# Four score rows in one arena, and the indexer's transposes and split moved ahead, in the first stage of a hybrid attention layer

## The chip, the cores and the metric

The kernel runs on one core of a Trainium2 chip. The metric is the device time of one execution in microseconds (us); lower is better.

## The reference

One layer over 4096 prompt frames and 8 streams of 16 new frames. A projection makes queries, keys, values and gates of two head groups and the queries, keys and weights of a small indexer. Group A attends in a sliding window. Group B attends, for each query, to the 256 keys that the indexer scores highest:

```
h = rms_norm(x, norm_g);  p = h @ w_in
qa, ka, va, ga, qb, kb, vb, gb, qi, ki, wi = split(p)
r = relu(einsum('bqhe,ble->bqhl', qi, ki_all))       # 4 indexer heads of 64
score = einsum('bqhl,bqh->bql', r, wi)               # -inf on chunks that are not admissible
_, idx = top_k(score, 256)
o_b = softmax(q . k[idx] / 8 + bias[idx]) . v[idx]
y = concat(o_a * silu(ga), o_b * silu(gb)) @ w_out;  x = x + y
```

## The kernel before, in words

The program has three stages, one behind the other: `stage_one` (projection, indexer scores, search of the 256th score, masks), `stage_two` (attention of the prompt) and `stage_last` (the samples and the output projection). The change is in `stage_one` alone and in the tables that order it.

Stage one handles 32 tiles of 128 prompt frames and one of samples. Each engine has one instruction stream that is written out by hand. A step t has 12 slots, and what an engine does in a slot is decided by comparing planned times: `us_at(t, slot)` is the planned time of a slot, and VectorE and ScalarE weave their two kinds of work by it. They have a foreground, the tests of a search, and a background (a generator that yields a planned time ahead of each piece); `advance` issues the background pieces whose planned time has passed. So the planned costs only set the order; at run time every engine works strictly in that order and waits on semaphores.

TensorE (PE) in step t: the scores of row u = t - 1 in units of 512 columns spread over slots 0 to 7 (`score_units`, L614: 4 heads of two matmuls a unit, into 4 banks), the transposes of the keys and queries of tile t - 1, and the projections of tile t (L596): k/v in slot 0, qa 2, qb 4, the index group 6; from tile 10 on the gates `ga` and `gb` in slots 8 and 10; from tile 23 on also the gates of an early tile (t - 23) in 9 and 11. In slots 5 and 7 it transposes the two halves of x of tile t + 1, and in slot 9 the index queries (L578) and index key (L581) of tile t. The key's bank is free only when ScalarE has copied the second half of x (L670).

ScalarE (ACT): evacuates each projection one slot later (L700; L698 for the index group), copies transposed pieces (L722, L725 for the index ones, in the slot behind theirs), takes the relu of the scores (L737, 3 buffers), and in its foreground searches the even rows with 31 tests over the whole row (L807).

GpSimd (POOL): weighs and adds the relus into the score row (L908 first head, L910 and L913 the others), marks the row ready with a memset (L917), and does the head norms.

VectorE (DVE): searches the odd rows with 32 tests (L1043), sums squares of heads (L946), splits the index query into a rounded part and a remainder (`split_q` L956, `split_k` L961; PE's scoring waits for both), and closes each row, even ones with the threshold that ACT found: a count (L993), two compares (L969, L970), a running sum over ties (L972), and two mask operations (L977, L980). The semaphore `s_fin` says that a close no longer needs its score row.

Score rows lie in three buffers, row a in `score[a % 3]`; POOL's first unit of row u waits until row u - 3 is closed:

```python
if j == 0 and u >= 5:
    pool.wait_ge(s_fin, u - 4)
```

Of the kernel before, what the change touches and what calls it, by code (L numbers as in the profile page):

```python
# [23 lines left out]
P = 128  # L24
# [101 lines left out]
N_PROJ = 2176  # L126
SLOTS = 12
RELU_GAP = 1.8
BIG = float(2 ** 100)
TESTS = 32  # L130
SEARCHED = TILES - 2
# [25 lines left out]
def unit_slot(u, j):  # L157

    return j * 8 // len(units(u))


SCORED = {}
# [47 lines left out]

def dve_us(t, slot):

    return 3.4 * (slot == 6) + 1.2 * (slot == 11) if t <= TILES else 0.0


def step_us(t):
# [67 lines left out]
def stage_one(nc, x_prompt, x_sample, norm_g, w_in, q_norm_a, k_norm_a, q_norm_b, k_norm_b,  # L284
# [3 lines left out]
    with ExitStack() as ctx:  # L288
# [14 lines left out]
        qi = sb("qi", [P, 2, IDX_HEADS * P], F32R)  # L303
        kiT = sb("kiT", [P, SEQ], F32R)
        relu = [sb(f"relu_{i}", [P, STEP]) for i in range(3)]
        score = [sb(f"score_{i}", [P, n]) for i, n in enumerate((31 * P, 32 * P, 30 * P))]
        mask = sb("mask1", [P, SEQ], BF16)
        ties = sb("ties", [P, 4 * PV], mybir.dt.int8)
        act_junk = sb("act_junk", [P, 31 * P], mybir.dt.int8)
# [22 lines left out]
        t_bank = [bank[:, (2 + i) * STEP:(3 + i) * STEP] for i in range(2)]  # L332
        s_bank = [bank[:, (4 + i) * STEP:(5 + i) * STEP] for i in range(4)]
        square = ties[:, :].bitcast(F32)
        bias_in, hot_in, ramp_sb = score[1][0:BUCKETS, 0:2 * HEADS], score[1][0:BUCKETS, STEP:STEP + 383], score[1][0:2 * HEADS, 2 * STEP:2 * STEP + 383]
        heads20 = proj[:, 0:PV].rearrange("p (h d) -> p h d", d=HD)

        s_const = sem("constants_loaded")
# [38 lines left out]
        block = ctx.enter_context(nc.Block())  # L377

        def row_of(a):
            return score[a % 3][:, 0:(a + 1) * P]  # L380

        @block.sync
        def _(sp):
# [67 lines left out]
            for t in range(TILES + 2):  # L451
                if t == 2:
                    sp.wait_ge(s_rampc, 1)
                    sp.dma_start(ramp[:, :, 0:RAMP - 1].rearrange("i h n -> h i n"),
                                 ramp_sb.unsqueeze(1).to_broadcast([2 * HEADS, P, RAMP - 1])).then_inc(s_ramps, 16)
                if t >= 1:
                    chosen_until(us_at(t, 1))
                    sp.wait_ge(s_tc, PIECE["k", t - 1] + 1)
                    from_ring(qk_t[t - 1, :, 2 * STEP:2 * STEP + 2 * P], P, 2 * P)
                    store_q(0, t - 1)  # L460
                if t < LATER:
                    sp.wait_ge(s_tc, PIECE["x1", t] + 1)
                    sp.dma_start(xt[t], x[t % 2][:, :]).then_inc(s_xt, 16)
                e = later_tile(t)
                if e is not None:
                    if e >= 1:
                        sp.wait_ge(s_pg, PROJ["gb", e - 1] + 1)
                    sp.dma_start(x_later[:, :], xt[e]).then_inc(s_xl, 16)
                if t <= TILES:
                    rows = slice(t * P, (t + 1) * P)  # L470
                    sp.wait_ge(s_ev, PROJ["kv", t] + 1)
                    sp.dma_start(values[t, :, 0:2 * P], proj[:, PV:PV + 2 * P]).then_inc(s_kv, 16)
                    if t < TILES:
                        sp.dma_start(b_v_prompt[0, 0].rearrange("t h d -> t (h d)")[rows], proj[:, PV + P:PV + 2 * P]).then_inc(s_kv, 16)
                    else:
                        sp.dma_start(b_v_sample[0].rearrange("b t h d -> (b t) (h d)"), proj[:, PV + P:PV + 2 * P]).then_inc(s_kv, 16)
                chosen_until(us_at(t, 4))
                if t >= 1:
                    store_q(1, t - 1)
                if t - 2 in LATE_TILES:  # L480
                    store_late(t - 2)
                if t > TILES:
                    continue
                chosen_until(us_at(t, 7))
                sp.wait_ge(s_ev, PROJ["idx", t] + 1)
                if t < TILES:
                    sp.dma_start(b_kidx_prompt[0, 0][rows], proj[:, PKI:PKI + HD]).then_inc(s_ki, 16)
                else:
                    sp.dma_start(b_kidx_sample[0].rearrange("b t d -> (b t) d"), proj[:, PKI:PKI + HD]).then_inc(s_ki, 16)
                chosen_until(us_at(t, 9))  # L490
                if t >= LATER:
                    sp.wait_ge(s_ev, PROJ["ga", t] + 1)
                    from_ring(gates[t, :, 0:STEP])
                if e is not None:
                    sp.wait_ge(s_ev, PROJ["ga", e] + 1)
                    from_ring(gates[e, :, 0:STEP])
                if t == TILES:
                    sp.wait_ge(s_tc, PIECE["iq", t] + 1)
                    from_ring(qi_new, HD)
                    sp.wait_ge(s_tc, PIECE["ik", t] + 1)  # L500
                    from_ring(ki_new, HD, P)
                sp.wait_ge(s_kn, t + 1)
                sp.dma_start(values[t, :, 2 * P:3 * P], proj[:, PK:PK + P]).then_inc(s_kv, 16)
                if t < TILES:
                    sp.dma_start(b_k_prompt[0, 0].rearrange("t h d -> t (h d)")[rows], proj[:, PK + P:PK + 2 * P]).then_inc(s_kv, 16)
                else:
                    sp.dma_start(b_k_sample[0].rearrange("b t h d -> (b t) (h d)"), proj[:, PK + P:PK + 2 * P]).then_inc(s_kv, 16)
                chosen_until(us_at(t, 11))
                if t + 2 <= TILES:
                    sp.wait_ge(s_pg, PROJ["gb" if t >= LATER else "idx", t] + 1)  # L510
                    if t < LATER:
                        sp.wait_ge(s_xt, 16 * (t + 1))
                    nxt = x_prompt[0, (t + 2) * P:(t + 3) * P] if t + 2 < TILES else x_sample.rearrange("b t d -> (b t) d")
                    sp.dma_start(x[t % 2][:, :], nxt).then_inc(s_x[t % 2], 16)
                if t >= LATER:
                    sp.wait_ge(s_ev, PROJ["gb", t] + 1)
                    from_ring(gates[t, :, STEP:2 * STEP])
                if e is not None:
                    sp.wait_ge(s_ev, PROJ["gb", e] + 1)
                    from_ring(gates[e, :, STEP:2 * STEP])  # L520
                if t == TILES:
                    sp.dma_start(a_k_sample[0, :, WINDOW - DEC:].rearrange("b t h d -> b t (h d)"), proj[:, PK:PK + P]).then_inc(s_last, 16)
                    sp.dma_start(a_v_sample[0, :, WINDOW - DEC:].rearrange("b t h d -> b t (h d)"), proj[:, PV:PV + P]).then_inc(s_last, 16)
                    sp.dma_start(wi_new, weight[:, t % 2, :]).then_inc(s_last, 16)
# [11 lines left out]
        def _(pe):  # L536
# [63 lines left out]
            def score_units(u, slot):  # L600

                for j, (c, n) in enumerate(units(u)):
                    if unit_slot(u, j) != slot:
                        continue
                    if j == 0:
                        pe.wait_ge(s_lo, 2 * u + 2)
                    for h in range(IDX_HEADS):
                        at = SCORED[u] + IDX_HEADS * j + h
# [11 lines left out]
            for t in range(TILES + 2):  # L620
                for slot in range(SLOTS):
# [9 lines left out]
                        transpose_q(1, t - 1)  # L631
                    if slot in (5, 7) and t < TILES:
                        transpose_x((slot - 5) // 2, t + 1)
                    if slot == 9 and t <= TILES:
                        transpose_indexer(t)
                    for at, name, of in groups_of_step(t) if t <= TILES else ():
                        if at == slot and slot > 0:
# [3 lines left out]
        def _(act):  # L641
# [97 lines left out]
            def background():  # L739
# [5 lines left out]
                for t in range(TILES + 3):  # L745
                    for slot in range(SLOTS):
                        before, b = divmod(SLOTS * t + slot - 1, SLOTS)
                        yield us_at(t, slot)
                        if b == 0 and 1 <= before <= TILES + 1:
                            copy_piece("k", before - 1)  # L750
                        for at, name, of in groups_of_step(before) if 0 <= before <= TILES else ():
                            if at == b:
                                evacuate(name, of)
# [5 lines left out]
                            copy_x((b - 5) // 2, before + 1)  # L759
                        if slot == 4 and t < TILES:  # L760
                            square_x(t + 1)
                        if b == 9 and before <= TILES:
                            copy_piece("iq", before)
                            copy_piece("ik", before)
                        if 3 <= t <= TILES:
                            for h, _ in enumerate(relu_unit(t - 1, slot)):
                                yield us_at(t, slot + 0.6) + RELU_GAP * h
# [92 lines left out]
        def _(pool):  # L860
# [31 lines left out]
            def add_scores(u, slot):  # L892
                last = len(units(u)) - 1
                for j, (c, n) in enumerate(units(u)):
                    if unit_slot(u, j) != slot:
                        continue
                    to = row_of(u)[:, c:c + n]
                    if j == 0 and u >= 5:
                        pool.wait_ge(s_fin, u - 4)
                    if j == 0 and u == 4:  # L900
                        pool.wait_ge(s_ramps, 16)
                    for h in range(IDX_HEADS):
                        at = SCORED[u] + IDX_HEADS * j + h
# [26 lines left out]
        def _(dve):  # L930
# [73 lines left out]
            def background():  # L1004

                taken = 2
                for t in range(TILES + 5):
                    for slot in (0, 3, 6, 9, 11):
                        while taken < SEARCHED and FOUND_AT[taken] <= us_at(t, slot):
                            yield FOUND_AT[taken]  # L1010
                            choose_act(taken)
                            taken += 2
                        if slot == 6 and t <= TILES:
                            yield us_at(t, slot)
                            sum_heads(t)
                        if slot == 11 and t < TILES:
                            yield us_at(t, 10.3)
                            split_q(t)
                            split_k(t)
                yield FAR_AWAY - 1  # L1020
                while taken < SEARCHED:
                    choose_act(taken)
                    taken += 2
# [1510 lines left out]
```

## Time and profile before

| | |
|---|---|
| time, median of 3 runs | 5097.78 us (5093.58 to 5100.38) |
| the profiled execution: its time, its span | 5096.76 us, 5095.0 us |
| first stage, from the start to the second stage's first instructions | 2456.4 us |
| busy, share of the span: PE, DVE, ACT, POOL | 85%, 69%, 68%, 32% |
| TensorE's granted clock, mean over the span | 0.92 of full speed |

A busy share is an average over all three stages. Idle time of an engine costs something only where another engine, or its own later work, waits for it. A wait that the trace puts down to "issue" is one whose releaser it does not show.

### The profile page before, as it was taken

To read this page: it belongs to the slowest core of one execution; us is meant where nothing else is said; L and a number is where in the kernel's file an instruction comes from. 1 tells how busy PE (TensorE), PEld (TensorE's weight loads), DVE (VectorE), ACT (ScalarE), POOL (GpSimd) and SP (SyncE) were. 2 spreads that over 40 slices of the span, in tenths; PEclk is the share of its full clock that TensorE was granted. 3 is DMA by queue.
4 is the path that set the end of the run, shared out by engine and by line. 5 is a ranking of instruction groups with operands and counts; after the bars stand their busy time and mean duration, and the time that the engine had idled before them with its cause. 6 is when DMAs were issued, how large, how long until landed. Compare 5 with 4: busy or idle time off the path is not lost. (4 is left out here: it accounts for less than half of the span.)

```text
span 5095.0 us, 78325 instructions
## 1 busy us (share of the span) xinstructions
PE 4347.4 (85%) x26505; PEld 2718.1 (53%) x26505; DVE 3499.8 (69%) x6644; ACT 3443.3 (68%) x6887; POOL 1619.9 (32%) x1358
## 2 busy tenths in 40 slices
PE   6777888777677786767689999989999999989999
PEld 3344444434343343434366777767777777754444
DVE  1277779888797898989477777787777778625111
ACT  1588888888787798872488888858788885520100
POOL 1345566667557757777210000000000000000000
PEclk8888889888788898978799999999999999999999
DMA  5211111100010111101421111011010010044422
GB/s 143 70 44 45 38 39 40 37 35 28 33 42 33 37 45 38 36 32 48 157 72 58 44 51 40 28 54 41 25 42 25 28 40 26 10 126 132 117 93 103
DMA packets 201975, 276.98 MB, mean 54 GB/s; under 512 B 50496, under 2 KB 134176, under 8 KB 201056
## 3 DMA queue, kind: packets, MB, share of 16 engines
q1 hardware_dynamic: 198624, 271.81, 16.9%
q8 instruction: 220, 3.60, 0.3%
q14 instruction: 171, 1.40, 0.1%
q10 hardware_dynamic: 2960, 0.17, 0.0%
HBM read 156.73 MB, written 114.16 MB: 53 GB/s over the span
## 5 line engine op out<-in xcount | busy, mean ns | idle before, releaser
L596 PE MATMUL bank<-w,x 128*128 128x512 f32 (+1 forms) x2848 | 1258.6, 598 | 19.2 <-DVE w L941 12.8
L1043 DVE TENSOR_SCALAR_CACHE_REDUCE ties<-score,cand 128x512 int8<-128x512 f32 (+13 forms) x448 | 1110.6, 2479 | 122.1 <-POOL score L917 106.7
L596 PEld LDWEIGHTS bank<-w,x 128*128 128x128 f32 x2848 | 576.9, 206 | 608.6 <-issue 549.7
L807 ACT ACTIVATE act_junk<-score,a_cand,a_sign 128x384 int8<-128x384 f32 (+13 forms) x420 | 879.4, 2094 | 14.0
L614 PE MATMUL bank<-kiT,qi 128*128 128x512 f32 (+3 forms) x1136 | 396.5, 489 | 450.5 <-ACT relu L737 244.9
L1834 DVE CUSTOM_DVE_ANT_0 row<-bank,mask 128x512 f32<-128x512 f32 (+3 forms) x1024 | 622.6, 639 | 181.6 <-PE bank L1573 180.3
L1540 POOL TENSOR_TENSOR near_bias<-table,mask 128x2048 f32<-128x2048 f32 (+1 forms) x32 | 129.5, 4047 | 1767.8 <-DVE part L1834 1751.4
L1768 ACT ACTIVATE pT<-bank 128x512 f32<-128x512 f32 (+2 forms) x704 | 368.4, 523 | 428.5 <-PE bank L1589 426.6
L1670 ACT ACTIVATE row<-row,top 128x1024 f32<-128x1024 f32 (+7 forms) x640 | 632.9, 990 | 4.0 <-DVE top L1847 4.0
L1573 PE MATMUL bank<-kT,qb 64*128 64x256 f32 (+1 forms) x4352 | 609.6, 397 | 9.0 <-DVE part L1834 5.6
L1589 PE MATMUL bank<-ident,row 128*128 128x128 f32 x4224 | 594.6, 281 | 26.4 <-DVE pT L1945 19.6
L1945 DVE COPY pT<-bank 128x512 f32<-128x512 f32 (+2 forms) x704 | 425.2, 604 | 255.8 <-PE bank L1589 254.2
L1618 PE MATMUL bank<-pT,v 128*64 128x128 f32 x8448 | 590.0, 280 | 0.0
L913 POOL TENSOR_TENSOR score<-score,relu 128x512 f32<-128x512 f32 (+3 forms) x426 | 560.3, 1315 | 33.4
L614 PEld LDWEIGHTS bank<-kiT,qi 128*128 128x128 f32 x1136 | 237.6, 232 | 578.3 <-ACT relu L737 307.0
L1618 PEld LDWEIGHTS bank<-pT,v 128*64 128x64 f32 x8448 | 450.9, 137 | 171.1 <-issue 163.7
L910 POOL TENSOR_TENSOR relu<-relu,weight 128x512 f32<-128x512 f32 (+3 forms) x426 | 499.3, 1172 | 76.9 <-ACT relu L737 76.7
L1589 PEld LDWEIGHTS bank<-ident,row 128*128 128x128 f32 x4224 | 453.1, 141 | 132.2 <-issue 97.0
L737 ACT ACTIVATE relu<-bank 128x512 f32<-128x512 f32 (+3 forms) x568 | 297.7, 554 | 252.1 <-POOL score L913 177.0
L2290 PE MATMUL bank<-wo,mix_in 128*128 128x512 f32 x1024 | 450.9, 599 | 0.0
L1573 PEld LDWEIGHTS bank<-kT,qb 64*128 64x128 f32 x4352 | 380.3, 187 | 125.5 <-issue 72.1
L908 POOL TENSOR_TENSOR score<-relu,weight 128x512 f32<-128x512 f32 (+3 forms) x142 | 164.6, 1159 | 651.4 <-issue 527.9
(255 smaller groups left out, 4900.1 us busy)
## 6 DMA issues: line engine op xcount, KB each, us to landing
qk_t<-ring SPq DMA_DIRECT2D x66, 256.0 KB, 2.0
gates<-ring SPq DMA_DIRECT2D x66, 256.0 KB, 2.0
gate<-gates SPq DMA_DIRECT2D x33, 512.0 KB, 3.4
out<-x_in SPq DMA_DIRECT2D x33, 512.0 KB, 2.9
x<-in_x_prompt SPq DMA_DIRECT2D x32, 512.0 KB, 3.7
mixed<-mixT SPq DMA_DIRECT2D x64, 256.0 KB, 2.0
mix_in<-mixed SPq DMA_DIRECT2D x32, 512.0 KB, 4.3
x_in<-in_x_prompt SPq DMA_DIRECT2D x32, 512.0 KB, 3.8
```

The source lines that it names most:

```text
L596: ins = pe.matmul(p_bank[n % 2][:, 0:n1 - n0], held[:, c * P:(c + 1) * P], w[:, c, n0:n1], start=(c == 0), stop=(c == KC - 1))
L614: ins = pe.matmul(s_bank[at % 4][:, 0:n], qi[:, part, h * P:(h + 1) * P], kiT[:, c:c + n], start=(part == 0), stop=(part == 1))
L807: tick(act.activation(junk, row, ACT.Sign, bias=c, scale=back, accum_out=a_sum[:, :]))
L910: k = tick(pool.tensor_tensor(r, r, weighs, ALU.mult))
L913: pool.tensor_tensor(to, to, r, ALU.add).then_inc(s_pa, 1)
L1043: n = tick(dve.tensor_scalar(ties[:, 0:width], row, c.bitcast(F32), 0.0, ALU.is_ge, ALU.add, accum_out=counts[:, i:i + 1]))
L1573: ins = pe.matmul(s[:, h * STEP + c0:h * STEP + c0 + m], qb[t % 2][half, g, :], kT[half, c + c0:c + c0 + m], start=True, stop=True)
L1589: ins = pe.transpose(t_bank[h][:, b * P:(b + 1) * P], held, ident[:, :])
L1618: ins = pe.matmul(oT[0 if k < 2 else 1][half * HD:(half + 1) * HD, col:col + P], value, pT[h][at % 2][:, b * P:(b + 1) * P], start=first, ...
L1670: act.activation(at, at, ACT.Exp, bias=bias, accum_out=out).then_inc(s_exp, 1)
L1834: ins = dve.tensor_tensor_reduce(row[k % 2][:, h, c0:c0 + w0], s[:, h * STEP + c0 - c:h * STEP + c0 - c + w0], more, 1.0, PAD, ALU.add, AL ...
L2290: ins = pe.matmul(y_bank[k % 2], held, w[:, c, i * STEP:(i + 1) * STEP], start=(c == 0), stop=(c == KC - 1))
```

## The change

It has five parts, all in stage one.

1. The three score buffers become one tensor, the arena, of 93 blocks of 128 columns. Row a begins at block `ROW_AT[a]`: up to row 19 four places 23 blocks apart are taken in turn, from row 20 on a table places each row. POOL waits, unit by unit, for the latest earlier row that overlaps that unit (`row_before`).
2. PE transposes the index pieces in slot 8 instead of 9, ahead of the gate group `ga`; ACT copies them one slot sooner, ahead of the evacuation of `ga`.
3. DVE's split is due at slot 9.3 instead of 10.3, and the closes that were taken up at slot 9 are now taken up at 7 or behind the split.
4. PE's first unit of a row waits for the split of the query alone, its last unit for that of the key.
5. In the sample's step two stores of index pieces go ahead of the gates' on SP's queue.

```diff
+SPLIT = 9.3
+ARENA = 93
+ROW_AT = {_a: _a % 4 * 23 for _a in range(2, 20)}
+ROW_AT.update(zip(range(20, TILES), (0, 24, 46, 69, 12, 37, 63, 0, 31, 63, 0, 31)))
+def row_before(u, c, n):
+    first, last = ROW_AT[u] + c // P, ROW_AT[u] + (c + n) // P
+    return max((b for b in range(2, u) if first < ROW_AT[b] + b + 1 and ROW_AT[b] < last), default=None)
...
-    return 3.4 * (slot == 6) + 1.2 * (slot == 11) if t <= TILES else 0.0
+    return 3.4 * (slot == 6) + 1.2 * (slot == 9) if t <= TILES else 0.0
...
-        score = [sb(f"score_{i}", [P, n]) for i, n in enumerate((31 * P, 32 * P, 30 * P))]
+        score = sb("score", [P, ARENA * P])
...
-            return score[a % 3][:, 0:(a + 1) * P]
+            return score[:, ROW_AT[a] * P:(ROW_AT[a] + a + 1) * P]
...
                     if j == 0:
+                        pe.wait_ge(s_lo, 2 * u + 1)
+                    if j == len(units(u)) - 1:
                         pe.wait_ge(s_lo, 2 * u + 2)
...
-                    if slot == 9 and t <= TILES:
+                    if slot == 8 and t <= TILES:
                         transpose_indexer(t)
...
+                        if b == 8 and 0 <= before <= TILES:
+                            copy_piece("iq", before)
+                            copy_piece("ik", before)
...
-                        if b == 9 and before <= TILES:
-                            copy_piece("iq", before)
-                            copy_piece("ik", before)
...
-                    if j == 0 and u >= 5:
-                        pool.wait_ge(s_fin, u - 4)
-                    if j == 0 and u == 4:
+                    before = row_before(u, c, n)
+                    if before is not None:
+                        pool.wait_ge(s_fin, before - 1)
+                    if j == 0 and u == 5:
                         pool.wait_ge(s_ramps, 16)
...
-                    for slot in (0, 3, 6, 9, 11):
-                        while taken < SEARCHED and FOUND_AT[taken] <= us_at(t, slot):
+                    for slot in (0, 3, 6, 7, SPLIT, 11):
+                        while slot != SPLIT and taken < SEARCHED and FOUND_AT[taken] <= us_at(t, slot):
...
-                        if slot == 11 and t < TILES:
-                            yield us_at(t, 10.3)
+                        if slot == SPLIT and t < TILES:
+                            yield us_at(t, SPLIT)
                             split_q(t)
                             split_k(t)
```

Three places of the built program show what moves. First DVE in tile 21's step, where it closes row 18 (2432 columns); before, from the row's first mask operations to the split:

```order
L970 TENSOR_SCALAR ties<-score_0,pick 128x2432
L972 SCALAR_TENSOR_TENSOR score_0<-ties 128x2432 [waits dve_ticks]
L975 SCALAR_TENSOR_TENSOR pick<-score_0,pick 128x1 [waits dve_ticks]
L977 SCALAR_TENSOR_TENSOR ties<-score_0,pick,ties 128x2432 [waits dve_ticks]
L980 SCALAR_TENSOR_TENSOR mask1<-ties,mask1 128x2432 [waits dve_ticks]
L956 TENSOR_TENSOR qi<-bank,qi 128x512 [waits dve_ticks,piece_copied]
L961 TENSOR_TENSOR kiT<-bank,kiT 64x128 [waits piece_copied]
```

The same place in the changed program:

```order
L1059 TENSOR_SCALAR ties,counts<-score,cand 128x2560 [waits dve_ticks]
L972 TENSOR_TENSOR qi<-bank,qi 128x512 [waits piece_copied]
L977 TENSOR_TENSOR kiT<-bank,kiT 64x128 [waits piece_copied]
L1005 TENSOR_SCALAR pick<-a_found 128x1 [waits act_found]
L1007 SCALAR_TENSOR_TENSOR pick<-a_found,pick 128x1 [waits dve_ticks]
L1009 TENSOR_SCALAR ties,pick<-score,pick 128x2432 [waits dve_ticks]
```

The two operations of the split now stand ahead of the whole close instead of behind it.

Second, PE at the end of the same step, before (L596 is a projection, here `ga` and then `gb`, L557 the transposes of x, L578 and L581 those of the index pieces, L614 the next row's scores):

```order
L557 MATMUL bank<-ident,x_0 128x128 x3
L596 MATMUL bank<-w,x_1 128x512 [waits group_evacuated]
L596 MATMUL bank<-w,x_1 128x512 x7
L578 MATMUL bank<-ident,proj 128x128 [waits group_evacuated,piece_copied]
L578 MATMUL bank<-ident,proj 128x128 x3
L581 MATMUL bank<-ident,proj 128x128 [waits piece_copied]
L596 MATMUL bank<-w,x_1 128x512 [waits group_evacuated]
L596 MATMUL bank<-w,x_1 128x512 x7
L614 MATMUL bank<-kiT,qi 128x512 [waits indexer_relu,indexer_split]
```

And in the changed program (L609 the projections, L591 and L594 the index transposes, L629 the scores):

```order
L570 MATMUL bank<-ident,x_0 128x128 x3
L591 MATMUL bank<-ident,proj 128x128 [waits group_evacuated,piece_copied]
L591 MATMUL bank<-ident,proj 128x128 x3
L594 MATMUL bank<-ident,proj 128x128 [waits piece_copied]
L609 MATMUL bank<-w,x_1 128x512 [waits group_evacuated]
L609 MATMUL bank<-w,x_1 128x512 x7
L609 MATMUL bank<-w,x_1 128x512 [waits group_evacuated]
L609 MATMUL bank<-w,x_1 128x512 x7
L629 MATMUL bank<-kiT,qi 128x512 [waits indexer_relu,indexer_split]
```

The index transposes, which wait for the index group's evacuation and for the copy of x, now stand ahead of both gate groups.

Third, ACT in the same step, before, with the gate's evacuation (L700), one search test (L811 to L807) and the two copies:

```order
L700 ACTIVATE ring_1<-bank,row_scale 128x512 [waits group_projected,ring_stored_1]
L811 ACTIVATE a_sign<-a_sum,a_sign 128x1 [waits act_ticks]
L780 ACTIVATE a_small<-a_sign 128x1 [waits act_ticks]
L780 ACTIVATE a_small<-a_small,a_const 128x1 [waits act_ticks]
L780 ACTIVATE a_cand<-a_const,a_small 128x1 [waits act_ticks]
L807 ACTIVATE act_junk,a_sum<-score_2,a_cand,a_sign 128x2688 [waits act_ticks]
L722 ACTIVATE qi<-bank 128x512 [waits piece_transposed,indexer_scored]
L725 ACTIVATE kiT<-bank 128x128 [waits piece_transposed]
```

And in the changed program:

```order
L822 ACTIVATE act_junk,a_sum<-score,a_const,a_sign 128x2688 [waits x_squared,act_ticks]
L737 ACTIVATE qi<-bank 128x512 [waits piece_transposed,indexer_scored]
L740 ACTIVATE kiT<-bank 128x128 [waits piece_transposed]
L715 ACTIVATE ring_1<-bank,row_scale 128x512 [waits group_projected,ring_stored_1]
L826 ACTIVATE a_sign<-a_sum,a_sign 128x1 [waits act_ticks]
```

The two copies went ahead of the gate's evacuation and of the test behind it; the tests themselves kept their places. On POOL the waits on `score_used` (the semaphore `s_fin`) went from 27, one a row, to 118, one for each unit that overlaps an earlier row.

## Rows read from the trace of the kernel before

**Rows 1.** Busy time by stretch, tiles 3 to 9, 10 to 22, 23 to 30:

```profile
core 0: us, PE busy (x) PEld busy (x) DVE busy (x) ACT busy (x) POOL busy (x), PEclk, DMA share, GB/s
190.00:530.00 340.00, 251.42 (x761) 138.64 (x761) 215.07 (x502) 294.43 (x712) 163.64 (x156) 0.85 0.14 47
530.00:1490.00 960.00, 734.04 (x2043) 391.50 (x2043) 815.34 (x1039) 805.42 (x1389) 617.14 (x511) 0.86 0.10 34
1490.00:2320.00 830.00, 629.73 (x1669) 328.56 (x1670) 728.10 (x631) 681.49 (x952) 570.91 (x462) 0.86 0.11 39
```

**Rows 2.** Waits of PE for the split, first two stretches (total us, times, longest):

```profile
PE bank L614 <- DVE kiT L961: 63.9, 7, 13.8
...
PE bank L614 <- DVE kiT L961: 123.0, 13, 22.1
```

**Rows 3.** Waits of ACT: first, second and third stretch:

```profile
ACT proj L700 <- PE bank L596: 25.6, 13, 4.9
...
ACT proj L700 <- PE bank L596: 37.3, 15, 6.3
...
ACT relu L737 <- POOL score L913: 81.7, 33, 11.8
```

**Rows 4.** Timeline, tile 21 (start, us, engine, line, operation, idle before):

```profile
1298.72 5.22 DVE L972 TENSOR_TENSOR_SCAN score<-ties 128x2432 f32<-128x2432 int8 x1
...
1307.14 2.69 DVE L980 SCALAR_TENSOR_TENSOR mask<-ties,mask 128x2432 bf16<-128x2432 int8 x1 [0.15 <-DVE ties L977]
1309.98 0.69 DVE L956 TENSOR_TENSOR qi<-bank,qi 128x512 fp32r<-128x512 f32 x1
...
1311.06 3.60 PE L614 MATMUL bank<-kiT,qi 128*128 128x512 f32 x8 [22.07 <-DVE kiT L961]
1312.31 0.60 ACT L737 ACTIVATE relu<-bank 128x512 f32<-128x512 f32 x1 [2.61 <-PE bank L614]
...
1321.86 0.69 ACT L700 ACTIVATE proj<-bank,row_scale 128x512 f32<-128x512 f32 x1 [6.30 <-PE bank L596]
```

**Rows 5.** Timeline of ACT behind odd tiles' splits, 11 and 19:

```profile
597.49 0.60 ACT L737 ACTIVATE relu<-bank 128x512 f32<-128x512 f32 x1 [3.31 <-PE bank L614]
...
1153.83 0.69 ACT L700 ACTIVATE proj<-bank,row_scale 128x512 f32<-128x512 f32 x1 [4.21 <-PE bank L596]
```

**Rows 6.** Timeline, ends of tile 12's and tile 26's steps:

```profile
640.67 8.73 PE L596 MATMUL bank<-w,x 128*128 128x512 f32 x16
...
645.08 0.67 ACT L700 ACTIVATE ring<-bank,row_scale 128x512 f32<-128x512 f32 x1
...
1781.42 0.48 PE L581 MATMUL bank<-ident,proj 128*128 128x128 f32 x1 [7.01 <-ACT x L670]
1781.69 8.86 PE L596 MATMUL bank<-w,x_later 128*128 128x512 f32 x16
1785.06 0.67 ACT L700 ACTIVATE ring<-bank,row_scale 128x512 f32<-128x512 f32 x1
...
1806.18 7.03 PE L596 MATMUL bank<-w,x 128*128 128x512 f32 x16
...
1816.96 0.70 ACT L700 ACTIVATE proj<-bank,row_scale 128x512 f32<-128x512 f32 x1
```

**Rows 7.** Timeline, POOL's adds and DVE around the close of row 29:

```profile
2387.17 1.03 POOL L910 TENSOR_TENSOR relu<-relu,weight 128x512 f32<-128x512 f32 x1
...
2399.22 8.88 DVE L972 TENSOR_TENSOR_SCAN score<-ties 128x3840 f32<-128x3840 int8 x1
2400.05 8.88 POOL L910 TENSOR_TENSOR relu<-relu,weight 128x512 f32<-128x512 f32 x1
```

**Rows 8.** Timeline, first add of row 31, and a wait near the stage's end:

```profile
2343.90 1.04 POOL L908 TENSOR_TENSOR score<-relu,weight 128x512 f32<-128x512 f32 x1 [24.53 <-issue]
...
2424.97 9.85 PE L596 MATMUL bank<-w,x 128*128 128x512 f32 x16 [6.33 <-ACT ring L700]
```

More of the change, by code:

```diff
@@ L334, in stage_one @@
         square = ties[:, :].bitcast(F32)
-        bias_in, hot_in, ramp_sb = score[1][0:BUCKETS, 0:2 * HEADS], score[1][0:BUCKETS, STEP:STEP + 383], score[1][0:2 * HEADS, 2 * STEP:2 * STEP + 383]
+        start = score[:, ROW_AT[5] * P:ROW_AT[6] * P]
+        bias_in, hot_in, ramp_sb = start[0:BUCKETS, 0:2 * HEADS], start[0:BUCKETS, STEP:STEP + 383], start[0:2 * HEADS, 2 * STEP:2 * STEP + 383]
         heads20 = proj[:, 0:PV].rearrange("p (h d) -> p h d", d=HD)
@@ L490, in _ @@
                 chosen_until(us_at(t, 9))
+                if t == TILES:
+                    sp.wait_ge(s_tc, PIECE["iq", t] + 1)
+                    from_ring(qi_new, HD)
+                    sp.wait_ge(s_tc, PIECE["ik", t] + 1)
+                    from_ring(ki_new, HD, P)
                 if t >= LATER:
@@ L496, in _ @@
                     from_ring(gates[e, :, 0:STEP])
[L497 to L501, printed above, removed]
                 sp.wait_ge(s_kn, t + 1)
```

## The prediction

> **What bounds the kernel now.** The page's slices put the only work that the diff touches, the first stage, into the first 2456 of 5095 us; the two later stages keep their instructions, so the whole change is read from the first. I read the stage's busy time by stretch first [rows 1]: in the three stretches ScalarE (ACT) is busy 294.4 of 340, 805.4 of 960 and 681.5 of 830 us, VectorE (DVE) 215.1, 815.3 and 728.1. Neither is full; the reader is to see that ACT, which has 46, 155 and 148 us to spare, works through one stream in which search tests, evacuations, copies and relus stand in a fixed order, so that each of its waits pushes all the rest back.
>
> Then the waits. PE waits for DVE's split of the index queries 63.9 us in the first stretch and 123.0 in the second [rows 2]. That looks like the prize, but it is PE's time. ACT waits for PE's projections 25.6 and 37.3 us, and in the third stretch its largest wait is for POOL's adds, 81.7 [rows 3]. So most of PE's stall is covered by ACT's own tests.
>
> Tile 21 shows how [rows 4]. DVE closes the search of row 18 (scan from 1298.72, last mask operation from 1307.14) and only then splits tile 21 (1309.98). PE has waited 22.07 us when scoring begins at 1311.06. ACT comes to its first relu 2.61 us before it can start, and then waits 6.30 us for the k/v projection behind the scoring: 8.9 us of ACT, not 22. The row-free semaphore never ends a wait here: the split stands behind the close that frees the row.
>
> **The change, part by part.** My sum is of waits added to or taken from ACT's stream.
>
> *Split ahead of the close; copies a slot sooner, tiles 3 to 9.* There are no gate groups yet, PE's order stays, and only ACT's copy and DVE's split move ahead. The seven waits of PE (63.9 us, about 9 each) exceed what ACT waits for PE (25.6 us in 13 waits, under 4 a step), so a start of scoring earlier by one ACT test and, in odd tiles, by one close covers most of it. I take three quarters: **-19 us** (bounds 0 and -25.6).
>
> *The same, odd tiles 11 to 21.* ACT's waits for PE behind the splits of 11 to 19 are five, 3.31 us the first and 4.21 the last, 14.6 together [rows 5]; with tile 21's 8.9 that is **-23 us** (bounds 0 and -43, the 37.3 us of [rows 3] with the relus' 2.61 and 3.31). DVE loses nothing by the order: the split's two operations cost the close about 1 us, and DVE waits on others elsewhere.
>
> *Transposes ahead of the gates, tiles 10 on.* Today the first gate group runs while ACT evacuates the index group and copies the second half of x; only then can PE do the transposes. Behind the change PE stands until that copy, and the gate group follows. In tile 12 the group behind the wait takes 640.67 to 649.40 us; ACT comes to its evacuation at 645.08, plus 0.9 for the two copies now ahead of it: a new wait of about 3.5 us. In tile 26 PE waits 7.01 us for the copy of x, the group then runs 1781.69 to 1790.55, and ACT is there at 1785.06 plus 0.9: 4.6 us [rows 6]. At the full pace of a group (7.03 us [rows 6]) these would be 2 and 3 us. Worked the same way, tiles 10 to 20 have seven such waits of 1 to 3.5 us, the other odd tiles none, since there the copy of x comes earlier: **+14 us** (bounds 9 and 21). Tiles 22, 26 and 28 have 3 to 4.6 us each: +12. The clock matters here by what the rows show: PEclk is 0.85 to 0.86 in all three stretches [rows 1], and a group behind a stall shows 8.73 or 8.86 us instead of 7.03 [rows 6].
>
> *Odd tiles 23 to 29.* Four gate groups follow the transposes there, and PE has no stall on the split to give back. PE instead ends its gates 6 us later in even tiles. The cover is thin: in tile 26 the next k/v projection runs from 1806.18 for 7.03 us and ACT evacuates it at 1816.96 [rows 6], 3.75 us of slack. Where ACT itself is late the slack holds, else 1 to 2.5 us is lost: +4. With the 12 above **+16 us** (bounds 5 and 30).
>
> *Four rows instead of three.* By the placement table rows 5 to 23 need the row four before them, but rows 29 and 31 overlap rows 26 and 28 from their first column. So row 31 gains little: its first add is at 2343.90 [rows 8], and it still needs row 28, which leaves DVE with the close. At the stage's end the sample's two copies take ring slots ahead of the gates, and PE already waits 6.33 us there for a ring evacuation [rows 8]; about 3 us each way: **0** (bounds -5 and +5). The 91 added waits of POOL on freed rows land on rows long free and cost nothing; if that cover went, one would cost what is left of a close, up to some 13 us (1298.72 to 1309.83 and its first part).
>
> Sum: -19 - 23 + 14 + 16 + 0 = **-12 us** on the profiled execution's own 5096.76 us: 5085 us. The median shown is 5097.78, 1 us above that execution, well inside the runs' 6.8 us.
>
> **A rule that speaks against it.** With the split ahead, POOL's adds of an odd row can fall into the close. The trace shows what that costs: an add that began at 2400.05 beside DVE's scan took 8.88 us, as long as the scan itself (8.88); the same add took 1.03 us at 2387.17 beside a search test [rows 7]. The Trainium skill, GPSIMD Engine Reference, section Specifications, says that POOL's SBUF interfaces are shared with VectorE and contended when a DVE instruction has two SBUF inputs or runs in a 2-port mode. The trace agrees for two inputs (8.88 us) and shows no cost beside the one-input test (1.03). By that rule the close's scan and mask operations would give an odd row no add before they end; it is rival B.
>
> **The rivals.** *A: PE's stall passes through whole.* If ACT's waits for POOL late in a step shrink with PE's earlier start, the gain is PE's: 63.9 less 3.5 in each of seven tiles for transposes, copy and split, -39; half of 123.0, -61; less 14 and 16 as above: -70, 5027 us. For it: DVE has waits too. Against it: in the third stretch ACT waits for POOL without any stall of PE. Chance 0.17.
>
> *B: the close holds POOL.* ACT reaches tile 21's first relu at 1309.7. Three relu buffers fill and the fourth waits for POOL, held to the end of the close, 1309.83 plus the split's 1 us. The waits for PE in odd tiles from 11 become waits for POOL and -23 shrinks to -7: +4, 5101 us. For it: rows 7. Against it: the last 2 us of the close alone overlap. Chance 0.17.
>
> *C: slower, by PE's wait for the copy of x.* If the gate evacuation is late by tile 26's 4.6 us in each of the eleven even tiles from 10 to 30 and by 1.5 in the odd ones, that is +51 +16, and with the 4 us behind them +71 against -42: 5126 us. It decides from about 2 us a tile over 22 tiles; I count 1.4. For it: PE slows behind a stall [rows 6]. Against it: odd tiles have the copy of x early. Chance 0.18.
>
> *That the change does nothing to order* is excluded: the rows of the program show all four moves.
>
> **How the numbers follow.** My forecast has 0.48, with its own range 5062 to 5105 from the terms' bounds taken two at a time. A measurement of this kernel can tell about 0.2%, 10 us. Of 0.48 some 0.29 is faster by more, 0.15 within, 0.04 slower; A is faster (0.17); B within 0.12, the rest split 0.03 and 0.02; C slower 0.16, within 0.02. Faster 0.49, same 0.29, slower 0.22. The range for 8 in 10 reaches from inside A to inside C: 5035 to 5115.
>
> **What would show it.** PE's wait for the split should fall from 187 us in the first two stretches to under 60. ACT's wait for the k/v projection in odd tiles should go. PE should wait more for ACT's copy of x ahead of the index-key transpose, and ACT for gate groups (ring evacuations), some 25 us in all. POOL's first add of row 21 should come at most 3 us earlier in its step, beside the close's last operations. The forecast is wrong if the third stretch gets shorter, if DVE's wait at the split grows past what its later waits take up, or if adds of 4 us and more appear at the start of odd rows.

## The result and the profile after

The changed kernel takes 5120.15 us (median of 4 runs, 5116.67 to 5121.68), the kernel before 5096.13 us in the same comparison (5093.58 to 5100.38): ratio 1.0049, 95% interval 1.0037 to 1.0062. It is 24 us slower, where 12 us less were forecast. The profiled execution has a span of 5119.9 us. Kernel times below are medians of runs; one of e11's five runs was slow (5139.45 us at a granted clock of 0.875 instead of 0.922 to 0.925) and is left out of its median and its ratio.

To see where the time went I cut stage one at instructions that the change does not move: ACT's evacuation of the qa projection of tile 10, of the k/v projection of tiles 16, 23 and 31, and of the last gate group. I call them marks. Between two of them ACT does the same work in both kernels. First the kernel before, by line and operation (durations, first and last start):

```profile
L700 ACT ACTIVATE proj<-bank,row_scale x1: 673/673/673, 495.2 to 495.2; 128x512 f32<-128x512 f32 x1
L700 ACT ACTIVATE proj<-bank,row_scale x1: 686/686/686, 859.1 to 859.1; 128x512 f32<-128x512 f32 x1
L700 ACT ACTIVATE proj<-bank,row_scale x1: 695/695/695, 1421.2 to 1421.2; 128x512 f32<-128x512 f32 x1
L700 ACT ACTIVATE proj<-bank,row_scale x1: 693/693/693, 2243.3 to 2243.3; 128x512 f32<-128x512 f32 x1
L700 ACT ACTIVATE ring<-bank,row_scale x2: 687/687/687, 2434.9 to 2441.8; 128x512 f32<-128x512 f32 x2
```

The same instructions of the changed kernel; the last group also shows what ACT waited for ahead of its four evacuations:

```profile
L715 ACT ACTIVATE proj<-bank,row_scale x1: 675/675/675, 484.7 to 484.7; 128x512 f32<-128x512 f32 x1
L715 ACT ACTIVATE proj<-bank,row_scale x1: 684/684/684, 864.0 to 864.0; 128x512 f32<-128x512 f32 x1
L715 ACT ACTIVATE proj<-bank,row_scale x1: 696/696/696, 1429.3 to 1429.3; 128x512 f32<-128x512 f32 x1
L715 ACT ACTIVATE proj<-bank,row_scale x1: 692/692/692, 2269.3 to 2269.3; 128x512 f32<-128x512 f32 x1
L715 ACT ACTIVATE ring<-bank,row_scale x4: 680/687/688, 2451.1 to 2467.5; 128x512 f32<-128x512 f32 x4
...
  DMA qi_new<-ring: 7.1, 1
```

So the change gains 10.5 us up to tile 10, loses 15.4 in tiles 10 to 15, 3.2 in 16 to 22, 17.9 in 23 to 30, and from 31 on nothing (198.5 and 198.2 us).

Next the waits of the changed kernel. PE, second stretch and then third, in the windows of [rows 1] (total us, times, longest):

```profile
PE bank L591 <- ACT proj L713: 51.1, 13, 11.3
PE bank L594 <- ACT x L685: 26.0, 9, 6.2
PE bank L629 <- DVE qi L972: 3.1, 2, 2.7
...
PE bank L591 <- ACT proj L713: 48.2, 5, 18.1
PE bank L594 <- ACT x L685: 30.0, 6, 7.4
```

ACT in the same two stretches:

```profile
ACT ring L715 <- PE bank L609: 27.4, 9, 5.6
ACT proj L715 <- PE bank L609: 18.9, 9, 5.0
...
ACT relu L752 <- PE bank L629: 0.4, 2, 0.2
...
ACT ring L715 <- PE bank L609: 15.6, 8, 5.1
```

Three readings. In the second stretch PE's wait for the split is all but gone (123.0 us in [rows 2], 3.1 now). ACT's wait for projections fell there from 37.3 [rows 3] to 18.9 as meant. But PE now stands ahead of the index transposes, first of all for the evacuation of the index group (L713), which the prediction did not price, and ACT waits 27.4 and 15.6 us for gate groups (`ring`).

Tile 17, an odd one, shows the new order (timeline):

```profile
968.05 0.79 ACT L713 ACTIVATE proj<-bank,row_scale 128x640 f32<-128x640 f32 x1
968.98 0.63 PE L591 MATMUL bank<-ident,proj 128*128 128x128 f32 x4 [3.28 <-ACT proj L713]
969.55 15.60 PE L609 MATMUL bank<-w,x 128*128 128x512 f32 x32
978.38 0.69 ACT L715 ACTIVATE ring<-bank,row_scale 128x512 f32<-128x512 f32 x1 [2.83 <-PE bank L609]
```

PE waits 3.28 us for the evacuation, does the transposes, and only then begins the gate group (the first 16 of the 32 records); ACT is there 2.83 us before its end. Tile 26 answers to [rows 6]:

```profile
1788.07 1.08 PE L591 MATMUL bank<-ident,proj 128*128 128x128 f32 x4 [16.30 <-ACT proj L713]
1796.16 0.48 PE L594 MATMUL bank<-ident,proj 128*128 128x128 f32 x1 [7.01 <-ACT x L685]
1796.43 8.65 PE L609 MATMUL bank<-w,x 128*128 128x512 f32 x16
1805.18 0.69 ACT L715 ACTIVATE ring<-bank,row_scale 128x512 f32<-128x512 f32 x1 [4.64 <-PE bank L609]
```

And tile 21, to [rows 4]: the split stands ahead of the close, scoring begins 5 us earlier and without a wait, and ACT's relu and the k/v evacuation behind it no longer wait for PE. ACT itself comes to that relu at 1320.10, where it came at 1309.70 before; so the two waits, 8.9 us, are all that the earlier scoring gives back in this tile.

```profile
1298.38 0.69 DVE L972 TENSOR_TENSOR qi<-bank,qi 128x512 fp32r<-128x512 f32 x1 [3.28 <-ACT qi L737]
1306.05 2.40 PE L629 MATMUL bank<-kiT,qi 128*128 128x512 f32 x8
1306.32 5.22 DVE L988 TENSOR_TENSOR_SCAN score<-ties 128x2432 f32<-128x2432 int8 x1
1320.10 1.55 ACT L752 ACTIVATE relu<-bank 128x512 f32<-128x512 f32 x3
1322.70 0.69 ACT L715 ACTIVATE proj<-bank,row_scale 128x512 f32<-128x512 f32 x1
```

### The profile page after: what moved, and what is told of

It reads as the page before. It is cut to its first block and busy times, and to the rows that moved or that the text cites. A ratio compares the mean times of both kernels' runs of the same rounds, so it can differ in the third digit from the quotient of the medians.

```text
span 5119.9 us, 78353 instructions
## 1 busy us (share of the span) xinstructions
PE 4369.3 (85%) x26505; PEld 2725.9 (53%) x26505; DVE 3493.0 (68%) x6644; ACT 3446.9 (67%) x6887; POOL 1628.6 (32%) x1358
## 5 line engine op out<-in xcount | busy, mean ns | idle before, releaser
L609 PE MATMUL bank<-w,x 128*128 128x512 f32 (+1 forms) x2848 | 1284.9, 609 | 29.9 <-ACT ring L715 17.5
L609 PEld LDWEIGHTS bank<-w,x 128*128 128x128 f32 x2848 | 592.1, 211 | 642.3 <-issue 574.9
L629 PE MATMUL bank<-kiT,qi 128*128 128x512 f32 (+3 forms) x1136 | 391.9, 481 | 339.5 <-ACT relu L752 292.0
L929 POOL TENSOR_TENSOR score<-score,relu 128x512 f32<-128x512 f32 (+3 forms) x426 | 573.8, 1347 | 33.4
L629 PEld LDWEIGHTS bank<-kiT,qi 128*128 128x128 f32 x1136 | 227.9, 223 | 467.4 <-ACT relu L752 353.7
```

The costliest lines, as they stand in the source:

```text
L609: ins = pe.matmul(p_bank[n % 2][:, 0:n1 - n0], held[:, c * P:(c + 1) * P], w[:, c, n0:n1], start=(c == 0), stop=(c == KC - 1))
L629: ins = pe.matmul(s_bank[at % 4][:, 0:n], qi[:, part, h * P:(h + 1) * P], kiT[:, c:c + n], start=(part == 0), stop=(part == 1))
L929: pool.tensor_tensor(to, to, r, ALU.add).then_inc(s_pa, 1)
```

## The experiments

Each ratio is to the kernel before on the same chip. "Stretch" is the time between the marks above.

**First round: which part costs.** Theory G says the transposes ahead of the gates, theory P the split ahead of the close.

*e3, the arena alone.* Everything but `ROW_AT`, `row_before` and POOL's wait goes back to the kernel before. 

> The kernel before with only the arena of score rows and GpSimd's new waits; split, transposes, copies and stores as before. Both theories: no change, 5096 us, range 5088 to 5102, since no add ever waited for a row. If four rows help by themselves, it is some 8 us less at row 31: 5088. If the 91 added waits of GpSimd cost, it is slower than 5104.

5095.31 us, ratio 1.0001 (0.9992 to 1.0010). The arena and its 91 added waits cost nothing and bring nothing that these runs can tell.

*e2, the split behind the close again:*

```diff
-                    for slot in (0, 3, 6, 7, SPLIT, 11):
+                    for slot in (0, 3, 6, 9, 11):
...
-                        if slot == SPLIT and t < TILES:
-                            yield us_at(t, SPLIT)
+                        if slot == 11 and t < TILES:
+                            yield us_at(t, 10.3)
```

> The changed kernel, but DVE's split stands behind the close again (slots, 10.3 and planner cost as before); transposes and copies stay one slot sooner. Theory G: the gate waits stay and ScalarE's waits for scoring and for the k/v projection in odd tiles come back (some 20 us): 5135 us, range 5125 to 5150. Theory P: the cost goes with the split, 5090 to 5105 us.

5128.66 us, ratio 1.0065 (1.0052 to 1.0078). Slower by 8.5 us than the changed kernel and inside G's range, though the step is little more than half of the 15 us of G's number. P, by which it had to be faster, falls in this form.

*e1, transposes, copies and the sample's stores behind the gates again from tile 10 on:*

```diff
-                    if slot == 8 and t <= TILES:
+                    if slot == (9 if t >= LATER else 8) and t <= TILES:
                         transpose_indexer(t)
...
+                        if b == 9 and LATER <= before <= TILES:
+                            copy_piece("iq", before)
+                            copy_piece("ik", before)
```

> The changed kernel, but from tile 10 on the index transposes, their copies and the sample's two stores stand behind the gates as before; the split stays ahead of the close. Theory G (the move ahead of the gates makes TensorE stand, and the first gate group then runs at the lower clock, which ScalarE waits for): the gate waits of tiles 10 to 30 (27 and 22 us) and the 8 us of tile 32 go, the gain of the early split stays: 5055 us, range 5045 to 5075. Theory P (the split ahead of the close costs, through GpSimd's adds and ScalarE's waits for them): nothing of it goes, 5105 to 5120 us.

5104.82 us, ratio 1.0019 (1.0010 to 1.0028). G's number is missed by 50 us (the 22 us that it gives to tiles 23 to 30 are 15.6 in the rows of the result), and the lower end of P's range is met. The gate waits went, and something else came: tiles 23 to 30 take 842 us, 20 more than before. The waits of DVE in e1, tiles 10 to 30:

```profile
DVE qi L975 <- ACT qi L737: 125.1, 16, 14.6
```

and in the kernel before, the same stretch:

```profile
DVE qi L956 <- ACT qi L722: 11.1, 5, 4.1
```

DVE works in order. With the split ahead of the close and the copies still late, the close stands behind the split's wait. In tile 25's step of e1 one sees how far that reaches (timeline):

```profile
1673.67 0.69 DVE L975 TENSOR_TENSOR qi<-bank,qi 128x512 fp32r<-128x512 f32 x1 [5.59 <-ACT qi L737]
...
1692.70 3.83 DVE L999 SCALAR_TENSOR_TENSOR mask<-ties,mask 128x2944 bf16<-128x2944 int8 x1 [0.15 <-DVE ties L996]
1696.61 0.32 SPq L447 DMA_DIRECT2D chosen<-mask  x1
...
1698.39 0.95 SPq L437 DMA_DIRECT2D gates<-ring  x2
...
1703.29 0.38 ACT L727 ACTIVATE ring<-bank 128x256 f32<-128x256 f32 x1 [9.16 <-DMA gates<-ring]
```

The close ends at 1696.5, SP stores its mask, and only behind that the gates; ACT waits 9.16 us for the ring slot that this store frees. Call this theory D. It is the only wait of that kind between the marks of tiles 10 and 31; most of what e1 loses reaches ACT as waits for POOL's adds and for projections (the table of ACT's waits below).

*e4, the old order for the sample's tile 32 alone* (as e1 with `TILES` for `LATER`). 

> The changed kernel, but for the sample's tile 32 alone the transposes, copies and the order of stores are as before. Theory G with the end as a cost of its own (a gate evacuation waits 7.1 us for the store of the index queries): 8 us less than the changed kernel, 5112 us. If the end only takes up what came late before it: 5120 us.

5114.09 us, ratio 1.0041 (1.0027 to 1.0055): 6 us of the loss lie in the sample's tile (from tile 31's mark on 190.8 us instead of 198.2). The run puts back transposes, copies and stores together; that it is the stores is read from the 7.1 us wait for `qi_new<-ring` shown above.

**Second round: keep the copies early, but not PE's transposes ahead of the whole gate group.**

*e5, transposes inside the gate group* (behind 4 of its 8 column blocks, tiles 10 to 31; tile 32 as in e4), and *e7*, behind 6:

```diff
                 for c in range(KC):
+                    if c == 4 and name == "ga" and not later and t < TILES:
+                        transpose_indexer(t)
                     ins = pe.matmul(p_bank[n % 2][:, 0:n1 - n0], held[:, c * P:(c + 1) * P], w[:, c, n0:n1],
```

> The changed kernel, but from tile 10 to 31 TensorE does the index transposes inside the first gate group, behind 4 of its 8 column blocks; the sample's tile 32 is as in e4. Theory G (the stall ahead of the transposes and the slow gate group behind it): the four blocks fill the stall, the group ends 3.5 us behind the transposes instead of 8.7, and ScalarE's waits for the gate (27 us in tiles 10 to 22, 15 in 23 to 30, 8 more than before in 31) go: 5065 us, range 5055 to 5080; at most 20 matmuls of first gate groups above 900 ns instead of 82. Theory D (the early split costs by VectorE's wait for the copies, 73 us where before had 11, and by what stands behind it): most comes back as waits for GpSimd, 5095 to 5112.

> As e5, but behind 6 of the 8 column blocks. Theory G: the copies come up to 1.8 us later where TensorE no longer stands, the gate waits are gone all the same: within 6 us of e5. Theory D: each us by which the copies come later is waited for by VectorE ahead of its close: 5 to 15 us more than e5.

e5: 5067.15 us, ratio 0.9945 (0.9931 to 0.9958). e7: 5058.37 us, 0.9927 (0.9914 to 0.9939), the lowest median of all and below both kernels. G's time was right for e5, whose waits for gate groups fell to 7.7 us between the marks of tiles 10 and 31 (48.1 in the changed kernel). Its side claim was not: 62 matmuls of e5's first gate groups in tiles 10 to 30 still took over 900 ns (78 in the changed kernel). So what went with the edit is the group's place, whatever the clock did.

*e8, only tiles under 10 as in the change; split behind the close everywhere.* 

> Arena; slot 8 for tiles under 10 alone, split behind the close everywhere, all else as before. If tiles 3 to 9 owe their 11 us to the copies and not to the order of the close: 5084 us, range 5080 to 5088. If the split ahead of the close is what gives it: 5092 to 5098.

5080.62 us, ratio 0.9967 (0.9954 to 0.9979). The gain of tiles 3 to 9 is the copies', not the split's.

*e6, each stretch with the order that did best in it.* 

> Arena; slot 8 for tiles under 10 and tile 31 alone, split ahead of the close for tiles under 10, 16 to 22 and 31, all else as before. If the stretches add up as measured (tiles 3 to 9 -11, 16 to 22 -7 with the split alone, 31 -8): 5069 us, range 5062 to 5078. If a gain in one stretch is lost in the next: 5080 to 5095.

5079.77 us, ratio 0.9966 (0.9954 to 0.9979). No better than e8: tiles 16 to 22 gained 9 us, and tiles 23 to 30, ordered as before, took 9.5 us more than before. In the trace that is ACT's wait for projections (30.2 us there, 21.6 before); why it grew stays open. Stretches do not simply add.

**Third round: what carries e7.**

*e11, as e7, but PE in the order of before from tile 10 on; only ACT's copies stand ahead of the gate's evacuation:*

```diff
-                    if slot == 8 and t <= TILES:
+                    if slot == (9 if t >= LATER else 8) and t <= TILES:
                         transpose_indexer(t)
...
-                        if b == 8 and 0 <= before <= TILES:
+                        if b == 8 and 0 <= before < TILES:
                             copy_piece("iq", before)
```

> As e7, but TensorE keeps the order of the kernel before from tile 10 on (transposes behind the whole first gate group); only ScalarE's two copies stand ahead of the gate's evacuation. If TensorE no longer stands anyhow and the copies' place is all that counts: within 4 us of e7, 5058. If two more column blocks (1.8 us) ahead of the transposes delay copies, split and close: 5064 to 5075 us.

5062.4 us, ratio 0.9938 (0.9924 to 0.9951), 4 us above e7, at the bound of the first case; the runs of the two overlap. Against e4 it moves only PE's transposes of tiles 10 to 31 back behind the gate group: 52 us less (58 less than the changed kernel, with the end). Against e1 it moves only ACT's two copies of a tile ahead of one evacuation: 42 us less. Its tile 26:

```profile
1750.99 0.47 PE L594 MATMUL bank<-ident,proj 128*128 128x128 f32 x1 [7.02 <-ACT x L685]
1751.26 8.43 PE L609 MATMUL bank<-w,x_later 128*128 128x512 f32 x16
1754.63 0.57 ACT L737 ACTIVATE qi<-bank 128x512 fp32r<-128x512 f32 x1
1755.27 0.68 ACT L715 ACTIVATE ring<-bank,row_scale 128x512 f32<-128x512 f32 x1
```

PE stands the same 7 us for the copy of x and the group behind it is as slow, but that is another gate group; ACT evacuates the first one, done long before, without a wait.

*e9, e7 with the split behind the close* (edit of e2). 

> As e7, but VectorE's split stands behind the close again. If the split ahead of the close is worth what the prediction's term said (23 us in tiles 11 to 21, and some 7 in tile 31): 5088 us, range 5080 to 5095. If it is worth only what the step from e2 to the changed kernel showed (8.5 us): 5067 us, range 5062 to 5073.

5083.23 us, ratio 0.9980 (0.9971 to 0.9989): the split ahead of the close is worth 25 us where its copies are early, 7 of them in tile 31. Without it e9 is within 1 us of the kernel before in every stretch from tile 10 on (table below): there the early copies give nothing by themselves.

*e10, e7 with the three score buffers and the wait for row u - 3.* 

> As e7, but with the three score buffers and the wait for the row three before, as in the kernel before. If the fourth row is what lets an odd row start beside the close: GpSimd's first add of an odd row waits for the close, ScalarE's relus behind it, and the gain of the early split goes: 5080 us, range 5070 to 5095. If the arena is nothing here either: 5058 us, range 5053 to 5064.

5061.37 us, ratio 0.9935 (0.9922 to 0.9947). Its runs (5058.48 to 5062.67) overlap e7's (5056.22 to 5063.38). My reason for a fourth row fell: it plays no part that these runs can tell.

*e12, e4 with the standing filled: ahead of the transposes PE does 6 column blocks whose sums are thrown away.*

```diff
+                    if slot == 8 and LATER <= t < TILES:
+                        fill(t)
                     if slot == (9 if t >= TILES else 8) and t <= TILES:
                         transpose_indexer(t)
```

> As e4 (5114 us), but ahead of the index transposes of tiles 10 to 31 TensorE does 6 of the first gate group's 8 column blocks, whose sums are thrown away, and behind the transposes the whole group as in the changed kernel: the order, the waits and the work behind the transposes stay, only the standing is filled. If the lower clock of the group behind the stand is the larger part of the gate waits: first gate groups fall from 8.7 to 7.5 us or less, and the time to 5095 us, range 5085 to 5104. If the place of the group (a whole group behind the transposes) is the larger part: 5108 to 5120 us.

5111.22 us, ratio 1.0031 (1.0018 to 1.0043), against 5114.09 for e4. First gate groups fell from 8.7 to 7.8 and 7.9 us (means over tiles 10 to 22 and 23 to 30), not to 7.5, and the time moved within the runs. It settles little: in tiles 11 to 30 the 20 fills take 108 us, more than the 88 us of standing that they took away, so they delay the transposes by about what the quicker groups give back.

## Why the prediction was wrong

The same stretches of seven kernels (us, from the marks above; the first column from the qa evacuation of tile 3, the last from tile 31's mark to the last gate evacuation):

| | 3 to 9 | 10 to 15 | 16 to 22 | 23 to 30 | 31 on |
|---|---|---|---|---|---|
| before | 321.5 | 363.9 | 562.1 | 822.1 | 198.5 |
| changed | 310.3 | 379.4 | 565.3 | 840.0 | 198.2 |
| e4: changed, tile 32 as before | 310.2 | 379.3 | 565.3 | 840.0 | 190.8 |
| e11: e4, PE's order as before | 310.4 | 360.8 | 548.3 | 824.1 | 190.9 |
| e7: transposes inside the group | 311.1 | 361.3 | 545.2 | 823.7 | 190.9 |
| e9: e7, split behind the close | 311.1 | 364.4 | 561.5 | 822.6 | 198.2 |
| e1: early split, late copies | 310.9 | 367.4 | 554.7 | 842.3 | 200.8 |

Between the marks of tiles 10 and 31 ACT is busy equally long in before, changed, e11 and e1 (1465 to 1468 us), so what it waits decides. The largest waits of the changed kernel and then of e11 (total us, times, longest):

```profile
ACT relu L752 <- POOL score L929: 132.9, 70, 12.6
ACT ring L715 <- PE bank L609: 43.0, 17, 5.6
ACT relu L752 <- POOL score L924: 42.6, 35, 6.1
ACT proj L715 <- PE bank L609: 37.6, 20, 5.0
...
ACT L715 <- PE bank L609: 5.1, 1, 5.1
...
ACT relu L752 <- POOL score L932: 120.7, 65, 12.6
ACT relu L752 <- POOL score L927: 41.7, 34, 6.1
ACT proj L715 <- PE bank L609: 41.3, 19, 5.0
...
ACT relu L752 <- PE bank L629: 8.9, 6, 6.7
```

The row of 5.1 us is tile 10's gate group; the trace puts its wait on the table load just ahead of the evacuation. All of ACT's waits by what ended them:

| ACT waits for (us) | before | changed | e11 | e1 |
|---|---|---|---|---|
| gate groups | 0.0 | 48.1 | 0.0 | 0.8 |
| other projections | 58.1 | 40.0 | 43.3 | 56.1 |
| scoring | 8.8 | 0.8 | 8.9 | 4.5 |
| POOL | 185.3 | 196.5 | 181.8 | 198.0 |
| a ring slot | 0.0 | 0.0 | 0.0 | 9.2 |
| sum | 252.2 | 285.4 | 234.0 | 268.6 |
| the stretch | 1748.1 | 1784.6 | 1733.1 | 1764.4 |

**The step that failed** is "Transposes ahead of the gates, tiles 10 on", with its share of tiles 22 to 30. With its tail of 4 us it was priced at +30; changed less e11 gives 18.6, 17.0 and 15.9 us in the three stretches, **+51**, and e4 less e11, which differ in PE's order alone, 52 us of the whole kernel. The mechanism was right: ACT waits for gate groups that stand behind the transposes, 48.1 us in the changed kernel and none in e11. The term was too small. I counted about 26 us in ten places; the trace has 48.1 in 18. 38.4 of them lie in the ten even tiles 10 to 28: tiles 10 to 20 wait 2.0 to 5.1 us where I had 1 to 3.5, tiles 22, 26 and 28 together 15.6 for 12, and tile 24 waits 2.7, which I had left out. The other 9.7 lie in odd tiles from 17 on. "The other odd tiles none, since there the copy of x comes earlier" failed there: PE stands for the evacuation of the index group instead (3.28 us in tile 17), and ACT waits (2.83 us). Where I had worked a tile out, it came close: 4.64 us in tile 26 for 4.6, 4.25 in tile 12 for 3.5. The 3 us between 48.1 and 51 are the other rows of the table: 15 more for POOL, 11 less for projections and scoring.

**Early tiles**: -11 instead of -19. I put it on the split and the close as well; e8 and e2 show it is the earlier transposes and copies alone (311 us in both, with the split behind the close).

**Odd tiles 11 to 21**: -23 forecast, -16.9 by e11 (tiles 10 to 22), -19 by e7 against e9 there. Near, but only for the pair: early copies with a late split give nothing (e9), an early split with late copies gives 4 us there and loses 20 in tiles 23 to 30 (e1). The reason beside it was not right: "DVE loses nothing by the order". DVE waited 73.5 us for the copies in the changed kernel (11.1 before), 125.1 in e1. In e11 (52.4) that is covered: between the marks of tiles 10 and 31 all of DVE's waits come to 219 us, 220 before. In the changed kernel they are 263 and in e1 258. In e1 the late close reaches SP, ACT and POOL, which is released by it twice (58.1 us in all).

**Four rows**: 0, and 0 measured (e3, e10). The end was 0 too, but as the sum of two: the sample's order costs 6 us (e4; 7 from tile 31's mark on), and the split of tile 31 gives 7 (e9 less e7 there: 198.2 and 190.9).

So -19 - 23 + 14 + 16 + 0 became, by stretches, -11.2 + 18.7 + 17.9 - 0.3 = +25.1. Early tiles (+8), odd tiles (+6) and gates (+21) all missed to the same side; my range took the bounds two at a time, as if they were independent.

**The rivals.** C is what happened in kind: it decides "from about 2 us a tile over 22 tiles", and 51 over 21 tiles is 2.4. That its 5126 us lies so near to 5120 is in part luck: it put the gates at 71 and the gains at 42, and measured are 51 and 28 (11.2 in the early tiles, 16.9 by e11). A fell: PE's wait for the split went from 187 us to 45.5 in the first two stretches, and only those 28 came through. B, the close that holds POOL, did not decide: ACT's waits for POOL grew by 11 us in the changed kernel and shrank by 4 in e11, which has the same split and is fast; 4 of 142 first operations of a unit took over 3 us, as many as before. The Trainium skill (GPSIMD Engine Reference, Specifications) says that POOL's SBUF interfaces are shared with VectorE and contended by a VectorE operation with two SBUF inputs. The trace agrees for the single add of [rows 7] (8.88 us); the runs show no such price in the total.

**The signs.** PE's wait for the split fell under 60 us, and PE waits more for the copy of x, as said (60 us between those marks, 36 before). ACT's wait for gates came, at twice its 25 us. Its wait for projections did not go, it fell from 58 to 40. DVE's wait at the split did grow past what its later waits took up, one of the signs named for a wrong forecast.

**What the lower clock costs stays open.** A first gate group behind the stand took 8.65 us in tile 26, at a mean granted clock of 0.81; the 7.03 us group of [rows 6] had 1.00. 1.6 us at 18 waits would be at most 29 of the 48 us. e5 and e12 changed the group's length or start as well, so neither isolates it. Part 4 of the change, PE's two waits for the split, stands in every run but e3 and was not tried alone.

## What to carry to other kernels

When a small operation is moved ahead of a large one in an in-order engine, price two things: the wait that it brings in front of the large one (between the marks of tiles 10 and 31 PE stood 164 us at the transposes, 63 before), and who waits for the large one's end. Try the consumer's side by itself: ACT's two copies ahead of an evacuation, together with the early split, gave what the change was good for (e11), without PE's move. Test the parts in pairs too: neither the copies nor the split gave it alone. Count a new wait in every tile and not only where the price is clearest, and let terms that hang on one assumption miss together in the range.

## What the runs showed that I had not expected

A wait placed on DVE reached ACT by SP's queue: mask store, then gate store, then the ring slot (9.16 us in e1's tile 25, once). And filling PE's standing with work did shorten the group behind it (8.7 to 7.8 us) without shortening the kernel.
